# Ten projections and sixteen gates per layer: high weights times high and low rows as one product of 512 columns, the halves added on VectorE

## What is computed

```python
def hybrid_mixer(h, w_in, w_branch_a, w_branch_b, b_gate, sink_logit, w_out):
    proj = jnp.einsum('bsd,dc->bsc', h, w_in)
    qa, ka, va, qw, kw, vw, gates = jnp.split(proj, SPLITS, axis=-1)
    oa = dilated_mixture(qa, ka, va)                 # 12 heads of 64, three dilations
    ya = jnp.einsum('bsc,cd->bsd', oa, w_branch_a)
    ob, _ = banded_attention(qw, kw, vw, ...)        # 16 heads, a window of 128
    yb = jnp.einsum('bsc,cd->bsd', ob, w_branch_b)
    g = jax.nn.sigmoid(gates + b_gate)
    return jnp.einsum('bsd,de->bse', g[:, :, 0] * ya + g[:, :, 1] * yb, w_out)
```

## Time and profile before

| | |
|---|---|
| median of 3 runs | 2141.39 us (2141.16 to 2141.56) |
| span of the profiled execution | 2141.5 us |
| PE busy | 1922.2 us, 90% |
| DVE busy | 643.6 us, 30% |
| ACT busy | 551.9 us, 26% |
| data moved by DMA | 748.67 MB, mean 350 GB/s |

### The profile page before, as it was taken

How to read it: one execution, slowest core, us unless ns; L and a number is a source line. 1 busy time by engine, 2 the same in 40 slices (tenths; PEclk the granted TensorE clock), 3 DMA queues, 4 the chain that set the end, 5 groups by cost and what they waited for, 6 DMA issues and landing times.

```text
span 2141.5 us, 32143 instructions
## 1 busy us (share of the span) xinstructions
PE 1922.2 (90%) x14286; PEld 1190.7 (56%) x14286; DVE 643.6 (30%) x984; ACT 551.9 (26%) x853; POOL 0.2 (0%) x4
## 2 busy tenths in 40 slices
PE   9999998787878999998888988889999998888887
PEld 8988833131312998872333433359999644444443
DVE  4476500000000548641431111057658200000001
ACT  4366300000000347530201222033544211111101
POOL 0000000000000000000000000000000000000000
PEclk9999999999999999999999999999999999999999
DMA  9734999999999962699999999974426999999996
GB/s 358 262 129 170 405 417 428 428 427 429 428 427 417 369 227 81 238 398 421 428 422 419 405 424 422 427 275 158 158 80 240 422 426 426 427 425 426 424 428 266
DMA packets 123037, 748.67 MB, mean 350 GB/s; under 512 B 6288, under 2 KB 27152, under 8 KB 83344
## 3 DMA queue, kind: packets, MB, share of 16 engines
q1 hardware_dynamic: 122896, 746.52, 85.4%
HBM read 745.45 MB, written 1.05 MB: 349 GB/s over the span
## 4 chain that ended last, share of the span: by engine, by line
PE 57%; DMA 35%; DVE 4%; ACT 2%; issue 1%; SPq 0%; DVEq 0%; ACTq 0%
PE bank L825 18%; DMA ring<-w_expert_up 11%; PE bank L916 11%; DMA ring<-w_expert_down 9%; PE bank L969 9%; PE bank L828 5%; DMA ring<-w_expert_gate 4%; DMA arena<-moe_w_up 4%; DMA ring<-moe_w_up 3%; DMA ring<-moe_w_down 2%; PE bank L947 2%; PE bank L852 2%; DMA arena<-moe_w_down 1%; PE bank L786 1%; PE bank L1120 1%
## 5 line engine op out<-in xcount | busy, mean ns | idle before, releaser
L916 PE MATMUL bank<-ring,arena 128*32 128x512 f32 (+1 forms) x3232 | 514.4, 509 | 85.1 <-DMA ring<-w_expert_up 40.9
L916 PEld LDWEIGHTS bank<-ring,arena 128*32 128x32 f32 x3232 | 164.2, 109 | 404.2 <-issue 209.5
L969 PE MATMUL bank<-ring,arena 128*32 128x512 f32 x1280 | 282.7, 612 | 47.2 <-DMA ring<-w_expert_down 38.7
L825 PE MATMUL bank<-arena_parts,ring_parts 128*128 128x256 f32 x1184 | 265.5, 283 | 0.0
L969 PEld LDWEIGHTS bank<-ring,arena 128*32 128x32 f32 x1280 | 69.4, 112 | 240.3 <-issue 171.8
L825 PEld LDWEIGHTS bank<-arena_parts,ring_parts 128*128 128x128 f32 x1184 | 198.5, 189 | 6.6 <-ACT arena_parts L1801 2.3
L1801 ACT ACTIVATE arena<-bank 128x512 f32<-128x512 f32 (+1 forms) x142 | 73.7, 544 | 451.1 <-PE bank L931 215.5
L2354 DVE TENSOR_TENSOR arena<-arena,bank 128x512 f32<-128x512 f32 x24 | 15.8, 685 | 553.3 <-PE bank L916 553.3
L825 PE MATMUL bank<-extra_parts,ring_parts 128*128 128x256 f32 x512 | 144.2, 282 | 0.0
L825 PE MATMUL bank<-ring_parts 128*128 128x256 f32 x672 | 127.5, 284 | 1.8 <-DVE arena_parts L2969 0.8
L825 PEld LDWEIGHTS bank<-ring_parts 128*128 128x128 f32 x672 | 105.7, 189 | 3.7 <-DVE arena_parts L2969 1.0
(11 more groups left out here) (394 smaller groups left out, 2444.6 us busy)
## 6 DMA issues: line engine op xcount, KB each, us to landing
ring<-w_expert_down SPq DMA_DIRECT2D x62, 2048.0 KB, 23.8
ring<-w_expert_gate SPq DMA_DIRECT2D x58, 2048.0 KB, 23.3
ring<-w_expert_up SPq DMA_DIRECT2D x54, 2048.0 KB, 25.6
ring<-w_in SPq DMA_DIRECT2D x32, 2048.0 KB, 11.5
ring<-moe_w_up SPq DMA_DIRECT2D x24, 2048.0 KB, 29.2
ring<-moe_w_gate SPq DMA_DIRECT2D x20, 2048.0 KB, 37.6
arena<-moe_w_down SPq DMA_DIRECT2D x16, 2048.0 KB, 34.0
ring<-ada_w SPq DMA_DIRECT2D x12, 2048.0 KB, 17.8
```

The source lines that it names most:

```text
L825: last = pe.matmul(out[:, n * S:(n + 1) * S], w[:, k, n * P:(n + 1) * P], x[:, k, :], start=first, stop=final)
L916: last = pe.matmul(to[own_rows(half, e)].rearrange("p (q c) -> p q c", c=own), x_slots[:, c, 32 * e:32 * e + 32], w[:, k, half], start=c = ...
L969: last = pe.matmul(banks[4 + e // PAIRS][own_rows(half, e), :].rearrange("p (x d) -> p x d", x=2), hidT[:, e // PAIRS * own + f % own, own ...
```

## The change

Jobs 1 to 5 (q and k), 9 to 12 (q of the window) and 13 (k of the window) and all gates get `pair_product`. High and low rows now lie side by side in `extra`, so one matmul streams both (2 x 256 columns) past the same high weights, into 512 columns of a bank: low rows' product left, high rows' product right. The low weights' product with the high rows is added to the right half as before. A block so has 8 matmuls of 512 columns and 8 of 256, where it had 24 of 256. The two halves are added outside PE: ACT copies (and scales) the right half, as before, and DVE adds the left one to it. A job takes a pair of banks, (0, 1), (2, 3) or (4, 5) in rotation. A gate's bank is now given back by DVE's add, `gate sum n`, and no longer by ACT's copy. The adds stand at fixed places in DVE's order. The table of distances moves to the place in `arena` that the high rows had, and in layer 1 its load waits for another, earlier step.

```diff
-IN_JOBS = [(n // 2, n % 2 * JOB, f"qk_dil {n}", "width", "act" if n < 3 else "dve") for n in range(6)] + \
+IN_JOBS = [(n // 2, n % 2 * JOB, f"qk_dil {n}", "width", "both" if n else "act") for n in range(6)] + \
...
+def in_bank(i):
+    return i % 3 * 2
...
+        hn_both = extra_parts[:, 0:UNIT].rearrange("p (x c t) -> p c x t", x=2, c=DC)
...
-        hn_high = parts(used[0], DC * S)
-        piece(DC * S)
+        hn_high = dists_parts.rearrange("p (c t) -> p c t", c=DC)
+        tables = piece(DC * S)
...
+            def pair_product(pair, high, low, src_both, src_high, weights=None, blocks=2):
+
+                outs = [pair[:, n * 512:(n + 1) * 512] for n in range(blocks)]
+                for n in range(blocks):
+                    for k in range(DC):
+                        pe.matmul(outs[n].rearrange("p (x t) -> p x t", x=2), high[:, k, n * P:(n + 1) * P], src_both[:, k],
+                                  start=k == 0, stop=False, skip_group_check=True)
+                        if not weights:
+                            last = pe.matmul(outs[n][:, S:2 * S], low[:, k, n * P:(n + 1) * P], src_high[:, k, :],
+                                             start=False, stop=k == DC - 1, skip_group_check=True)
...
+                def in_job(i):
+                    unit, _, step, way, _ = JOBS[i]
+                    out = pair_of(i) if way == "width" else take(in_bank(i), "act", step)
...
                 def gate(n):
...
-                    out = take(next_bank(), "act", step)
+                    out = take(next_bank(), "dve", f"gate sum {n}")
...
-                    split_product(out, gate_high[n % GATE_BUFS], gate_weights(n, ring_parts), hn_high, hn_low, blocks=1)\
+                    pair_product(out, gate_high[n % GATE_BUFS], gate_weights(n, ring_parts), hn_both, hn_high, blocks=1)\
...
-                    act.activation(gates[:, n, :], next_bank()[:, 0:S], ACT.Identity, bias=par[:, at:at + 1])\
+                    act.activation(gates[:, n, :], next_bank()[:, S:2 * S], ACT.Identity, bias=par[:, at:at + 1])\
...
+                        copy(step, rows_of(i), high_half(i), scale_of(i))
...
+                def gate_add(n, turned):
+
+                    gate_turn[0] += 1
+                    bank = banks[1 + gate_turn[0] % 3]
+                    gate_turn[0] += turned
+                    dve.wait_ge(act_done, act_at(f"gate {n}", loops))
+                    dve.tensor_tensor(gates[:, n, :], gates[:, n, :], bank[:, 0:S], ALU.add)\
+                       .then_inc(dve_done, dve_p.mark(f"gate sum {n}"))
...
+                            last = dve.scalar_tensor_tensor(rows_of(i), low_half(i), scale_of(i), rows_of(i), ALU.mult, ALU.add)
...
                 gate_low(2)
                 dil_scores(0, 0)
                 gate_low(3)
+                gate_add(0, 0)
                 dil_scores(0, 1)
                 dil_probs(0, 0)
                 gate_low(4)
+                gate_add(1, 0)
+                gate_add(2, 0)
                 dil_scores(1, 0)
                 dil_probs(0, 1)
+                gate_add(3, 2)
                 gate_low(5)
                 dil_scores(1, 1)
                 dil_probs(1, 0)
+                gate_add(4, 2)
                 gate_low(6)
                 gate_low(7)
                 dil_probs(1, 1)
+                gate_add(5, 2)
                 win_scores(0)
                 gate_low(8)
+                gate_add(6, 2)
                 gate_low(9)
                 win_scores(1)
                 gate_low(10)
+                gate_add(7, 0)
                 for w in range(pairs):
                     win_probs(w)
                     if w >= 2:
...
                         win_scores(w + 2)
                     if DC + w + GATE_BUFS < len(GATE_JOBS):
                         gate_low(DC + w + GATE_BUFS)
+                    gate_add(DC + w, 2)
...
-                            sp.wait_ge(dve_done, dve_at("mix 3", loops, layer=1))
-                        sp.dma_start(dists[:, 0:DIST_COLS], io["consts"][:, C_DIST:C_COLS]).then_inc(dist_loaded, 16)
+                            sp.wait_ge(pe_done, pe_at("tile_0 unit 12", loops, layer=1))
+                        sp.dma_start(tables[:, 0:DIST_COLS], io["consts"][:, C_DIST:C_COLS]).then_inc(dist_loaded, 16)
```

More of the change, by code:

```diff
@@ L404, in build @@
         n_passes = sb("n_passes", 1, I32)
-        banks = [ctx.enter_context(nc.psum_tensor(f"bank{i}", [P, 512], F32)) for i in range(8)]
+        with ExitStack() as first_view:
+            banks = [first_view.enter_context(nc.psum_tensor(f"bank{i}", [P, 512], F32)) for i in range(8)]
+        bank_pairs = [ctx.enter_context(nc.psum_tensor(f"bank_pair{i}", [P, 2 * 512], F32)) for i in range(4)]
         h3 = hT[:].rearrange("p (c t) -> p c t", c=DC)
@@ L413, in build @@
         rms_root, rms_inv = rms[:, 0:S], rms[:, S:2 * S]
-        dil_dist = [dists[:, half * DIL_KEYS:(half + 1) * DIL_KEYS] for half in range(TH)]
-        win_dist = dists[:, TH * DIL_KEYS:DIST_COLS].rearrange("p (q k) -> p q k", q=TH)
         def in_order(rows):
@@ L776, in first_product @@
                                          stop=part_of == "rest" and k == DC - 1, skip_group_check=True)
+                return last
+            def pair_product(pair, high, low, src_both, src_high, weights=None, blocks=2):
[7 more added lines that the diff above has]
+                                             start=False, stop=k == DC - 1, skip_group_check=True)
+                if weights:
+                    weights()
+                    for n in range(2):
+                        for k in range(DC):
+                            last = pe.matmul(outs[n][:, S:2 * S], low[:, k, n * P:(n + 1) * P], src_high[:, k, :],
+                                             start=False, stop=k == DC - 1, skip_group_check=True)
                 return last
@@ L1096, in _, with pair_of @@
                     sum_squares_part("norm1", squares, j, norm_bank, "squares")
+                def pair_of(i):
+                    first = in_bank(i)
+                    for bank in (first, first + 1):
+                        out = take(bank, "dve", JOBS[i][2])
+                    return bank_pairs[first // 2]
+                def in_job(i):
+                    unit, _, step, way, _ = JOBS[i]
+                    out = pair_of(i) if way == "width" else take(in_bank(i), "act", step)
+                    pe.wait_ge(dve_done, dve_at(f"low {i}", loops))
+                    low = job_weights(JOBS[i], ring_parts)
+                    steps = [step] + ([unit_done(unit)] if JOBS[i + 1][0] != unit else [])
+                    last = pair_product(out, high_room(i), low, hn_both, hn_high) if way == "width" else \
+                        split_product(out, high_room(i), low, hn_high, hn_low, way)
+                    last.then_inc(pe_done, pe_p.mark(*steps))
                 def job(i, src_high, src_low, ready=None):
                     unit, _, step, way, reader = JOBS[i]
-                    out = to_act(step) if reader == "act" else to_dve(step)
+                    out = to_dve(step)
                     pe.wait_ge(dve_done, dve_at(f"low {i}", loops))
@@ L1253, in _ @@
                     if i > 1:
-                        job(i, hn_high, hn_low)
+                        in_job(i)
                     elif i:
@@ L1989, in _ @@
                     if reader == "act":
[L1990 to L1996 removed]
+                        bank = two(banks[in_bank(i)])
+                        if not i:
+                            copy(step, rows_of(i), bank, scale_of(i))
+                        else:
+                            copy(step, v_dil[:, :, JOB * (i - 6):JOB * (i - 5)] if step != "v_win" else v_win, bank)
+                    else:
+                        copy(step, rows_of(i), high_half(i), scale_of(i))
                     if i == 7:
@@ L2615, in _ @@
                         gate_low(i + 2 - len(IN_JOBS))
+                    if reader == "both":
+                        dve.wait_ge(act_done, act_at(step, loops))
+                        if step == "k_win":
+                            for kv in range(2):
+                                rows = slice(kv * HD, (kv + 1) * HD)
+                                for r in range(2):
+                                    last = dve.tensor_tensor(k_win[r * HD:(r + 1) * HD, kv:kv + 3:2, :], low_half(i)[rows],
+                                                             k_win_part[rows], ALU.add)
+                        else:
+                            last = dve.scalar_tensor_tensor(rows_of(i), low_half(i), scale_of(i), rows_of(i), ALU.mult, ALU.add)
+                        last.then_inc(dve_done, dve_p.mark(step))
                 def ada_cols(step, bank, out):
```

50 lines of the change are left out of this document (24 added, 26 removed).

## The result

The changed kernel takes 2172.76 us (median of 4 runs, 2167.37 to 2175.13) and the kernel before, run beside it, 2141.47 (4 runs, 2141.16 to 2142.78): ratio 1.0138, 95% interval 1.0125 to 1.0152. It is 31 us slower; 22 was forecast. The profiled run took 2173.36 us and has a span of 2171.6, 30.1 more than before.

A forecast was written before the change was run, and what follows sets the result against it. PE, busy 90% of the span, was taken to bound the kernel; per layer -3.2 - 2.4 + 11.8 + 4.9 = +11.1 us, two layers +22 on 2141.5, giving 2164 us, 1.0% slower; 8-in-10 range 2152 to 2176.

The forecast's parts named there:

- the waits: Attention gates: PE stands until DVE's add frees the bank, 3.3 + 4.0 + 3.0 + 1.5 = 11.8 us lost per layer.
- rival (e): Window rounds: DVE is too late in every round as well, 0.5 us or more each; 2172 us and above; chance 0.07.
- (c): Gate 4: PE does not stand, gate 3's add being done in time; only savings count, 2130 us; chance 0.08.
- (d): Behind the head: the delay is swallowed because DMA bounds the experts; about 2141 us; chance 0.04.
- the clock: After the three long waits at gates 4, 5 and 7 the granted clock falls to 0.50: 4.9 us per layer.
- The mean of the earlier trace: Clock after nine idle PE stretches: mean 0.66 over the next 5 us, 1.7 us lost each, taken as 1.6.
- the upper bound that I gave: Clock term: at most 2.5 us lost behind each of three long waits per layer; lower bound 0.
- Rival (a): Attention: the waits are there but the clock holds; 2154 us; chance 0.18.
- I take 215.8: Projections and gates: a 512-column matmul costs 215.8 ns, 19.8 under two narrow ones; bounds 213.5 and 235.6.
- rival (b): Projections and gates: the wide product costs as much as two narrow ones; 2175 us; chance 0.13.
- -3.2 and -2.4 a layer: PE savings per layer from wide products: 3.2 us in ten projection jobs, 2.4 us in 15 of 16 gates.
- the likeliest case: Stalls at the gates with the low clock: 2164 us, its own range 2157 to 2171; chance 0.50.

The follow-up runs named there:

- experiment 2: Changed kernel with DVE's adds of gates 3, 4, 6 and 8 moved earlier in DVE's order: 2146.82 us, ratio 1.0023 to the kernel before.
- experiment 3: Changed kernel with 17, 17 and 12 throwaway products on PE before gates 4, 5 and 7: 2164.55 us, ratio 1.0106 to the kernel before.
- The experiment on bare rates: Changed kernel with nine runs of throwaway matmuls before layer 0's attention: 512 columns 229 ns, 256 columns 118; the kernel's time means nothing.
- Experiment 5: Changed kernel with gates as before and each wide projection product issued as two narrow ones: 2137.86 us, ratio 0.9977 to the kernel before.
- experiment 6: Wide products before narrow ones in each block: on experiment 2, 2144.87 us; on the changed kernel with gates as before, 2136.45 us.
- experiments 5 and 8: The second of these: Experiment 5 with the products of jobs 1 and 2 wide again, 128 instructions shorter: 2135.7 us, ratio 0.9966 to the kernel before.

## Why the prediction was right, and where not

**Right: the waits.** Forecast were 4.0, 4.0, nothing, 3.0 and 1.5 us at gates 4, 5, 6, 7 and 9, a sum of 11.8 with the 0.7 that goes away. Measured are 4.03, 4.03, none, 3.08 and 1.45, in layer 0 and again in layer 1, 12.6 in all, and the 0.68 of the earlier trace rows is gone. Counting whose turn the bank is, and adding up DVE's list to the add from the earlier trace rows, was exact to 0.1 us at each gate. The add itself takes 0.41 us (0.42 forecast). The rounds of the window wait for nothing, so rival (e) did not occur; moving the adds (experiment 2) takes the long waits and the low clock away, and with them 13.9 of the 19.0 us of layer 0; filling the waits (experiment 3) leaves 12.35 of them, which is what the waits alone come to. Rivals (c) and (d) fall too: `yb` starts 18.6 us later in layer 0 and 34.7 in layer 1, and from there to the last stage next to nothing is given back (-0.2 us in the ledger).

**Right in kind, too low: the clock.** The forecast had 1.6 us for each of three waits, 4.9 a layer. With the waits filled, layer 0 gets 6.7 us and layer 1 4.4 us: 11.1 in two layers against 9.8. The mean of the earlier trace rows was too mild for layer 0: gate 4 takes 133.80 - 128.31 = 5.49 us for what was 3.03, 2.5 more, which is the upper bound that I gave. In layer 1 gates 4, 5 and 7 take 4.39, 4.36 and 4.32 us from their first matmul to what follows, in layer 0 5.29, 4.55 and 5.42, against 2.9 to 3.0 with the waits filled: behind gate 4 the clock is back sooner, behind gate 7 it falls later. Rival (a) is out.

**Wrong: "I take 215.8".** The step that failed is the inference that 117.8 ns is nearer to the weight load than to the columns, and that a wide product therefore costs only its stream, which I took to be as long as that of an fp32 matmul of 256 columns. The experiment on bare rates puts it at 229 ns alone, with half the weights no less, and the gates at 235.6 in turn with a narrow one. That is my upper bound, rival (b)'s price. The 16 pairs of each of ten jobs save nothing but 0.05 to 0.1 us in job 1 and, in layer 1 alone, 0.36 us in the window's jobs, and the gates nothing: -3.2 and -2.4 a layer, 11.2 in all, are next to 0. The inference had a weak base that could be seen beforehand: the rows of plain fp32 hold two records for each product that the kernel issues (16 rows for the 8 products of L1523, 32 for the 16 of L1538; experiment 3's 92 small products leave 184). So 215.8 ns is the distance between two records, each half of a product, and not what any one product costs. The Trainium skill's page "TensorE: Matmul & The Clock Gate", section "Back-to-back issue gap", which I set against my rows, gives N / 2.4 + 2.5 ns: 215.8 for 512 columns and 109.2 for 256, where the runs have 229 and 118. Its size is low, but what I worked out from it, that merging two products saves next to nothing, is right, and I gave that 13%. My reason for setting it aside, that it leaves the load out, fails: half the load changes 117.8 to 116.6 ns.

**Not seen.** The projections do end earlier, 1.1 and 0.8 us a layer, mostly for another reason: narrow matmuls run faster in some jobs, in layer 0 above all the token jobs (v's and the last one, whose products have the rows as weights; 114.9 ns and not 120.0), which the change leaves as they are but for where their operands lie. Experiment 5 has these gains and more without a wide product. That the places of the operands do it is not shown, and alone they do not: experiment 6 has the same places and loses a part of the gain, and in experiments 5 and 8 the same jobs in the same places go at two rates. The cause stays open. And the last stage gives 4.3 us back, by where its loop lies in the program.

**The sum, again, with measured terms:** waits 2 x (12.6 - 0.7) = 23.8, clock 11.1, further small waits of the attention 0.9 (the ledger's 35.8 less those two), projections -1.9, last stage -4.3, start and all else +0.5. That is 30.1, by which the spans differ. Of the 0.9, 0.7 are two waits of 0.35 us for ACT late in the attention (L1250), which I had not counted. The time of rival (b) was 2175, and measured are 2172.8: it was (b) that came, with 1.2 us a layer too little for waits and clock, and 6.2 us that came back unseen. The time lies inside the range of 8 in 10 but not in the likeliest case's own, and that it lies inside is luck: without the 4.3 us of the last stage, which have nothing to do with the forecast's mechanism, it would be 2177, above the range.

## What to carry to other kernels

Before merging two matmuls into a wide one, find what the distance of the narrow ones consists of by changing one operand at a time (columns, weight columns), since a rate inferred from another data type was wrong by all that was to be gained. When the reader of a buffer changes, count whose turn each buffer is and add up the new reader's list to the release: that was exact here, and it decided. And when a stage that was not touched changes its time, look at the instruction queue's transfers before you look for a cause in the work.

The faster kernel of this study is the one with the gates as before (2135.15 and 2136.18 us); 4 to 5 of its 6 us come from where the loop lies.

## What the runs showed of the hardware

- 256-column fp32r matmuls with a full load of weights each go at 113.3 to 120 ns from start to start, 512-column ones at 229, 384-column ones at 173; half the weight columns change the 256-column one from 117.8 to 116.6. The same narrow job goes at 114.9, 119.2 or 120.0 ns in different kernels; in two that differ only in the jobs ahead of it, another one goes at 115.4 and 119.9. The cause stays open.
- A granted clock of 0.50 followed all six idle stretches of 3.08 and 4.03 us, sometimes at once (128.31), sometimes 0.8 us of work later (139.84: two pairs of 0.45 and 0.37 us, then 0.64 us each), and none of the waits of up to 1.81 us in experiment 2's layer 0. The wait of 3.28 us behind which the earlier trace rows had it at 1.00 (1424.36) is there in the changed kernel too, also of 3.28 us (at 1458.09), and there the clock is 0.52 over the next 2 us: the length of a wait does not settle it.
- A plain fp32 matmul of the kernel leaves two matmul records in the trace, one of fp32r leaves one (184 records for 92 products; 240 for 240).
- A loop whose instructions are fetched again in every pass waits 4.5 to 5.1 us at each jump back (in one run 6.2 and 6.5), where 3.07 are there anyway, and takes some 30 transfers of 16 KB over its three jumps; 126 instructions more ahead of it were enough to switch that on, 128 fewer to switch it off.
